# A transformer block on one core: gates of the second merge as filling work, and attention scores over the whole array

## The reference, cut to what matters

```python
for l in range(DEPTH):                       # 2 layers
    h = rmsnorm(x, norm_w[l])
    proj = h @ w_in[l]                       # q_b k_b v_b z_b gate_a gate_b ...
    y_a = gated_delta_branch(...)
    y_b = diff_attention_branch(q_b, k_b, v_b, z_b, ...)
    merged = sigmoid(gate_a) * (y_a @ w_pa[l]) + sigmoid(gate_b) * (y_b @ w_pb[l])
    x = x + merged @ w_out[l]

# diff_attention_branch, for each of 8 heads:
    q, k = partial_rope(q), partial_rope(k)  # two maps of 64 channels
    s = einsum('nbhqd,nbhkd->nbhqk', q, k)   # n = the map
    p = softmax(s)
    o = (p[0] - lam * p[1]) @ v
    y = rmsnorm(o, subln_w) * (1 - lambda_init) * silu(z)
```

## Time and profile before

| | |
|---|---|
| median of three runs | 3010.39 us |
| profiled execution | 3007.67 us |
| its span, first to last instruction | 3005.9 us |
| PE busy | 2952.6 us, 98% of the span |
| DVE, ACT, POOL busy | 57%, 47%, 15% |
| granted PE clock over the span | 0.999 |
| DMA, share of 16 engines | 22.7% in the queue of the loads |

### The profile page before, as it was taken

One profiled execution on the slowest core, in us unless ns is written; L12 is line 12 of the kernel. 1 busy time (PEld: TensorE's weight loads), 2 busy tenths in 40 slices (PEclk: granted clock), 3 DMA queues, 4 the chain that ended last, 5 costly groups with the idle time before them and its releaser, 6 DMA issues. The chain is left out here.

```text
span 3005.9 us, 51504 instructions
## 1 busy us (share of the span) xinstructions
PE 2952.6 (98%) x20584; PEld 2374.7 (79%) x20584; DVE 1716.1 (57%) x2610; ACT 1426.2 (47%) x2807; POOL 451.2 (15%) x288
## 2 busy tenths in 40 slices
PE   9999999999999999999999999999999999999999
PEld 6788788777787777877777877778888777788887
DVE  7766743776447777634676446554444555544443
ACT  4555543666334555534665345653223356632322
POOL 1555530000013445410000020000000100000000
PEclk9999999999999999999999999999999999999999
DMA  4121122212222112122221322212222222122222
GB/s 152 65 78 54 62 78 86 76 60 74 84 89 86 65 65 86 34 95 74 74 76 44 107 102 77 82 68 101 98 96 86 84 88 78 41 107 96 86 97 84
DMA packets 42692, 243.22 MB, mean 81 GB/s; under 512 B 6833, under 2 KB 7793, under 8 KB 17137
## 3 DMA queue, kind: packets, MB, share of 16 engines
q1 hardware_dynamic: 42480, 240.30, 22.7%
HBM read 233.36 MB, written 2.20 MB: 78 GB/s over the span
## 5 line engine op out<-in xcount | busy, mean ns | idle before, releaser
L320 PE MATMUL bank<-hT,ws 128*128 128x512 f32 x2112 | 875.6, 415 | 8.0 <-ACT rq L3182 2.5
L324 PE MATMUL bank<-hT,ws 128*128 128x512 f32 x2112 | 826.6, 391 | 0.0
L323 PE MATMUL bank<-hT,ws 128*128 128x512 f32 x2112 | 824.5, 390 | 0.0
L271 ACT ACTIVATE ws<-raw 128x2048 fp32r<-128x2048 f32 x172 | 328.8, 1912 | 296.1 <-PE bank L320 181.1
L320 PEld LDWEIGHTS bank<-hT,ws 128*128 128x128 f32 x2112 | 397.4, 188 | 91.0 <-issue 12.7
L324 PEld LDWEIGHTS bank<-hT,ws 128*128 128x128 f32 x2112 | 396.4, 188 | 87.1
L277 DVE TENSOR_TENSOR ws<-raw,ws 128x2048 fp32r<-128x2048 f32 x156 | 363.6, 2331 | 161.8 <-ACT ws L271 158.5
L323 PEld LDWEIGHTS bank<-hT,ws 128*128 128x128 f32 x2112 | 398.2, 189 | 66.8 <-issue 1.4
L1213 PE MATMUL bank<-uS,ws 128*128 128x512 f32 x512 | 199.2, 389 | 0.0
L1216 PE MATMUL bank<-uS,ws 128*128 128x512 f32 x512 | 199.2, 389 | 0.0
L1217 PE MATMUL bank<-uS,ws 128*128 128x512 f32 x512 | 199.2, 389 | 0.0
(11 more groups left out here) (388 smaller groups left out, 4887.2 us busy)
## 6 DMA issues: line engine op xcount, KB each, us to landing
raw<-in_w_ff SPq DMA_DIRECT2D x64, 1024.0 KB, 4.7
raw<-in_w_delta SPq DMA_DIRECT2D x32, 1024.0 KB, 4.7
raw<-in_w_diff SPq DMA_DIRECT2D x32, 1024.0 KB, 4.7
raw<-in_w_att SPq DMA_DIRECT2D x20, 1024.0 KB, 4.7
raw<-in_w_merge_a SPq DMA_DIRECT2D x16, 1024.0 KB, 4.8
raw<-in_w_merge_b SPq DMA_DIRECT2D x16, 1024.0 KB, 4.7
raw<-in_w_out SPq DMA_DIRECT2D x16, 1024.0 KB, 4.8
rows<-sum_rows SPq DMA_DIRECT2D x16, 512.0 KB, 5.7
```

What stands on the lines that cost most here:

```text
L271: act.activation(self.k.ws[:, c % 2, 0], self.k.raw[:, c % 2], ACT.Copy).then_inc(self.high_done, 1)
L320: first = pe.matmul(out, hi, x[:, 0, k], start=(begin and k == steps[0]), stop=False)
L323: pe.matmul(out, hi, x[:, 1, k], start=False, stop=False)
L324: last = pe.matmul(out, lo, x[:, 0, k], start=False, stop=(end and k == steps[-1]))
```

## The change

The scores become two matmuls per map over the full array: the stationary side holds a map's query high part in one half of the rows and its low part in the other (`QS`), the moving side the key's high part in both halves (`KH`), then the key's low part in both (`KL`). Two things follow. Splits of queries and keys are written in halves of 64 partitions, two instructions each where there was one. And six transfers of 64 x 512 fp32 per head put the parts into the other half of the partitions (`place_query`, `place_key`). The low parts now stand ahead of `weights` on DVE, the high parts ahead of the raw copies on ACT.

The filling work changes its counts: 28 steps, 9, then 7, so 44 steps are done when unit 0 begins. At its end it now holds four gate tiles at the full rate, copied to `gt`, and 7 steps of each of the first two `w_pb` tiles. The chunks of the merge are reordered (`MERGE_B_ORDER`), and chunk (1,0) and (1,1) are split inside the diff phase, the low part of (1,1) on POOL. `last_merge_phase` replaces `merge_phase`.

```diff
-GATES_AHEAD = 6
+MERGE_B_ORDER = ((0, 0), (0, 2), (1, 0), (1, 2), (0, 4), (1, 4), (0, 6), (1, 6))
+GATES_AHEAD, GATES_AHEAD_B = 6, 4
...
 @block.gpsimd
                 pool.memset(rot[:, :, :], 0.0).then_inc(cleared, 1)
+                following.low(pool, 1, 1)
...
 @block.sync
+                def place_query(h):
+                    sp.wait_ge(qk_ready, nth(h, 2, 0))
+                    for m in range(2):
+                        sp.dma_start(QS[MAPS[1 - m], h % 2, m].bitcast(F32), ql[MAPS[m]].bitcast(F32)).then_inc(placed[0], 16)
+                def place_key(h):
+                    sp.wait_ge(qk_high, nth(h, 2, 1))
+                    for m in range(2):
+                        sp.dma_start(KH[MAPS[1 - m], h % 2, m].bitcast(F32), KH[MAPS[m], h % 2, m].bitcast(F32)).then_inc(placed[1], 16)
+                    sp.wait_ge(qk_ready, nth(h, 2, 1))
+                    for m in range(2):
+                        sp.dma_start(KL[MAPS[1 - m], h % 2, m].bitcast(F32), KL[MAPS[m], h % 2, m].bitcast(F32)).then_inc(placed[1], 16)
...
                 for h in range(1, HEADS):
                     swap(h, 0)
                     refill(h, 1)
                     swap(h, 1)
+                    place_query(h)
+                    place_key(h)
                     if h + 1 < HEADS:
                         refill(h + 1, 0)
-                following.load_after(sp, 0, 0)
+                for n in range(4):
+                    following.load_after(sp, n // 2, n % 2)
...
 @block.tensor, stream()
-                    for _ in first_gates(k, pe, following, taken, 4 * HEADS):
+                    following.credit(pe)
+                    for n in range(GATES_AHEAD_B):
+                        x = n // 2
+                        if n % 2 == 0:
+                            following.ready(pe, 0, x)
+                        pe.wait_ge(taken, 4 * HEADS + n - 1)
+                        for last in following.product(pe, B[n % 2][:, :], x, n % 2, k.hT):
+                            if last is None:
+                                yield
+                        last.then_inc(tile, 1)
                         yield
-                        yield
-                    pe.wait_ge(p_ready, 2 * UNITS1)
-                    yield from first_merge(k, pe, following, MERGE_DIFF, yS, lambda t: pe.wait_ge(ylo, t + 1))
+                    following.ready(pe, 1, 0)
+                    for m in range(2):
+                        pe.wait_ge(taken, 4 * HEADS + GATES_AHEAD_B + m - 1)
+                        part = following.product(pe, B[m][:, :], 0, m, yS, steps=MERGE_FIRST, end=False)
+                        for t in MERGE_FIRST:
+                            pe.wait_ge(ylo, t + 1)
+                            next(part)
+                            yield
...
 @block.tensor, scores(u)
                     if n == 0:
                         pe.wait_ge(qk_ready, nth(h, 2, 1))
+                        pe.wait_ge(placed[0], 32 * (h + 1))
+                        pe.wait_ge(placed[1], 64 * (h + 1))
...
-                    for t, (a, b) in enumerate(((0, 0), (0, 1), (1, 0))):
-                        for m in range(2):
-                            hp = slice(64 * m, 64 * (m + 1))
-                            last = pe.matmul(B[SB + m][:, :], qk[hp, h % 2, 0, a, n * P:(n + 1) * P], qk[hp, h % 2, 1, b],
-                                             start=(t == 0), stop=(t == 2))
+                    for m in range(2):
+                        q = QS[:, h % 2, m, n * P:(n + 1) * P]
+                        pe.matmul(B[SB + m][:, :], q, KH[:, h % 2, m], start=True, stop=False)
+                        pe.matmul(B[SB + m][:, :], q, KL[:, h % 2, m], start=False, stop=True).then_inc(s_ready, 1)
...
                 fill = stream()
                 some(fill, 3 * KT + 4)
+                turn_v(0)
+                some(fill, KT + 1)
                 scores(0)
-                some(fill, KT - 4)
-                turn_v(0)
-                some(fill, KT)
+                some(fill, KT - 1)
...
 @block.scalar, in the loop over units
+                    if n in (1, 2) and more:
+                        qk_high_part(h + 1, n - 1)
                     if n < 3 and more:
                         raw_copy(h + 1, n)
-                    if n in (1, 2) and more:
-                        qk_high_part(h + 1, n - 1)
+                    elif not more:
+                        gate_copy(n)
...
+                    if n == 2 and not more:
+                        following.high(act, 1, 0)
...
                         if more:
+                            z_gate(h + 1)
                             v_turned(h + 1)
-                            z_gate(h + 1)
...
                 out_rms(HEADS - 1)
+                following.high(act, 1, 1)
                 high_part(HEADS - 1)
...
 @block.vector, in the loop over units
+                    if n in (1, 2) and more:
+                        qk_low_part(h + 1, n - 1)
                     if n == 1 and h > 0:
                         norm_out(h - 1)
                     if u + 1 < UNITS1:
                         weights(u + 1)
...
-                    if n in (1, 2) and more:
-                        qk_low_part(h + 1, n - 1)
...
+                    if n == 2 and not more:
+                        following.low(dve, 1, 0)
```

More of the change, by code:

```diff
@@ L391, in weight_chunks @@
             f.append(tile_pair(column_tile(w, (COL_VB + at, P)), column_tile(w, (COL_ZB + at, P))))
[L392 to L395, removed]
+        for chunks, order, sides in ((ma, MERGE_A_ORDER, ((w, COL_GA), (pa, 0))), (mb, MERGE_B_ORDER, ((w, COL_GB), (pb, 0)))):
+            for side, n in order:
+                m, at = sides[side]
+                chunks.append(tile_pair(column_tile(m, (at + n * P, P)), column_tile(m, (at + (n + 1) * P, P))))
         for n in range(0, KT, 2):
@@ L856, in gated_merge_phase, with last_merge_phase @@
     k.next_phase()
[L859 to L878, removed]
+def last_merge_phase(k, st, following, yS, macc, gt, mS, pairs=()):
     st.open()
@@ L881, in merge_phase @@
                                               "constants_loaded")
[L882 to L962, removed]
@@ L2426, in _ @@
                 swap(0, 1)
+                place_query(0)
+                place_key(0)
                 refill(1, 0)
@@ L2547, in raw_copy, with gate_copy @@
                     act.sem_inc(raw_ready, 1)
+                def gate_copy(n):
+                    act.wait_ge(tile, 4 * HEADS + n + 1)
+                    act.activation(gt[:, n], B[n % 2][:, :], ACT.Copy).then_inc(taken, 1)
                 def v_turned(h):
@@ L2556, in qk_high_part @@
                     act.wait_ge(qk_mixed, nth(h, 2, j))
-                    act.activation(qk[:, h % 2, j, 0], rq[:, j], ACT.Copy).then_inc(qk_high, 1)
+                    for m, hp in enumerate(MAPS):
+                        ins = act.activation((QS, KH)[j][hp, h % 2, m], rq[hp, j], ACT.Copy)
+                    ins.then_inc(qk_high, 1)
                 def z_gate(h):
@@ L2639, in qk_low_part @@
                     dve.wait_ge(qk_high, nth(h, 2, j))
-                    dve.tensor_tensor(qk[:, h % 2, j, 1], rq[:, j], qk[:, h % 2, j, 0].bitcast(F32), ALU.subtract).then_inc(qk_ready, 1)
+                    if j == 0 and h > 0:
+                        dve.wait_ge(placed[0], 32 * h)
+                    for m, hp in enumerate(MAPS):
+                        low = KL[hp, h % 2, m] if j else ql[hp]
+                        ins = dve.tensor_tensor(low, rq[hp, j], (QS, KH)[j][hp, h % 2, m].bitcast(F32), ALU.subtract)
+                    ins.then_inc(qk_ready, 1)
                 def maxes(u):
```

140 lines of the change are left out of this document (122 added, 18 removed).

## The result

The changed kernel takes 3107.5 us (median of 5 runs, 3103.6 to 3109.9), the kernel before 3011.3 beside it (3008.7 to 3013.1): a ratio of 1.032, 95% interval 1.0309 to 1.0332. That is 96 us slower; the forecast was 61 us slower, with a range up to 3100, so the time lies outside the range. The span of the profiled execution rose from 3005.9 to 3102.9 us, by 97.0.

What follows compares the result with a forecast made beforehand. PE, busy 98% of the span, was taken to bound the kernel. The terms -5 + 55 - 4.5 + 10 + 8 = +63.5 us on 3007.67 gave 3071, stated as 3072 us for the median; range 3042 to 3100.

Steps and rivals of the forecast that it cites:

- The wait in block 2: PE waits for the chunk's low part on DVE, 4.0 us in heads 1 to 6, 3.4 in head 0: +55 us.
- S: Start of the last filling matmul ahead of a unit's scores, from which the forecast counts times in that unit.
- Rival 2, the clock falls: PE returns at 1.2 GHz behind 16 waits, 2.8 us each: +45, about 3117; in a third, 3087; chance 0.12.
- Scores: Four full-array matmuls replace six paired half-row ones, saving 0.08 us per unit over 64 units: -5 us.
- the bound of -10: Far bound of the scores' saving, if the turning matmul also starts without its extra delay.
- Last head: PE's old waits at half-rate gates go, -4.5 us; new waits for merge chunks in blocks 0 and 2, +10 us.
- Phase boundary: At the barrier PE waits 5 us instead of 1, behind ACT's and POOL's late chunk (1,1): +8 us for both.
- At nothing: Priced at zero: key transfers covered by block 2's wait (+20 at most without it); block 3's silu gate in time.
- Rivals 1 and 3: Block 2: 1, only the softmax chain delays the chunk, about 3042, chance 0.2; 3, no wait, about 3000, 0.06.
- rival 1's 8.0: Block 2's chunk low part ends 8.0 us after S if DVE is free and only the softmax stands in the chain.

Runs made afterwards that it cites:

- forty: The changed kernel with 40 instead of 44 filling steps ahead of unit 0: 3007.7 us, ratio 0.9993.
- before_44: The kernel before the change with 44 instead of 40 filling steps ahead of unit 0, nothing else: 3112.1 us, ratio 1.0341.
- split_first: The changed kernel, 44 steps kept, with the chunk's low part in block 2 right behind the maxima on DVE: 3036.7 us, ratio 1.0087.
- best_old_scores: The changed kernel with 40 steps, ACT's chunk (1,1) split before the norm, raw copies first, but old half-array scores and no transfers: 3007.8 us.
- warm_half: The changed kernel with seven idle fp32 products on PE in the block 2 waits of heads 0 to 6: 3101.6 us, ratio 1.0306.

## Why the prediction was wrong

- **The wait in block 2, +55: right.** Measured 56.2. S + 4.7 for the reciprocal, 6.3 for the gating, 9.6 for the end of the low part were all met; head 0 waits 3.73, heads 1 to 6 3.74 to 4.42. forty and before_44 show the cause by taking the four steps out and putting them in, split_first by moving the low part.
- **The clock, left out of the sum: the step that failed.** "Rival 2, the clock falls" was given 0.12 and the sum nothing, on the ground that the longest wait of the trace, 2.48 us, kept the full clock. That row was one draw: the same wait lost the clock in four of twelve traces. It also says nothing of waits of 4 and 5 us, and falls followed the last heads' waits of 2.3 to 2.5 us too. The page of the Trainium skill weighed there ("TensorE: Matmul & The Clock Gate", part 1) said that idling halves the clock, and the trace now agrees: 0.53 and 0.64 in the windows behind the wait. The sum should have held a term for it. Its size in the rival (2.8 us for each of 16 waits, +45) was too high, because the lower clock held for part of the twelve matmuls only, 1.61 us in the wait shown; there were 20 such waits, and the estimate from the mean clock is 34 in all. The other terms came to 61.4 where 63.5 was summed, and 3072 + 34 = 3106 is 1.5 us under the measured 3107.5. A match that close is partly luck, since the 34 is good to some 3 us only.
- **Scores, -5: under-sized.** -8 by the distances: 0.07 us of it to the turning matmul, as forecast, and 0.05 behind it, which was named only as the bound of -10. best_old_scores bears it out, though its two differences (10.8 and 7.0) are too far apart to fix the size.
- **Last head, -4.5 and +10: right** (10.2).
- **Phase boundary, +8: right in size** (7.5), in part by luck. POOL's operation took 4.51 us and not the 4.95 reckoned with, and DVE's last one, 4.06 us long beside it, ended 0.56 us later still; the two nearly cancel. I had written "a collision could lengthen it" and priced nothing.
- **At nothing:** the transfers were indeed hidden behind the waits. Without that cover they cost 2.4 us (forty) to 8.3 (split_first), not up to 20, and nothing where the raw copies come first. The silu gate was hidden in the changed kernel; in before_44, with ACT's old order, it cost 5.7.
- **Rivals 1 and 3** are out: the rotation of the key ended at S + 1.2, not before S, and DVE reached the low part at S + 7.3, not before 3.3. What put its end 1.6 us above rival 1's 8.0 was mostly ACT, not DVE: from the maxima (731.65) to the exponentials (733.78) were 2.13 us instead of 0.73, since the key's high parts and raw copy stand between. The forecast had that order in its chain.
- **A slip of the sum.** 3071 and 2.7 for the median are 3074, not 3072. It changes nothing here.

What stays open: what decides whether the clock falls behind a wait of 2 to 3.6 us. It isn't the length alone, nor the work around the wait: the same code kept the clock in one execution and lost it in another, and no run here shows on what that hangs.

## What to carry to other kernels

When filling work is consumed in portions and the lead ahead of the loop isn't a whole number of units, count for every portion in which unit it begins and where its preparation stands on the other engines there; four steps more in that lead, one number, were worth 100 us here. With that number right the change was worth 3 us against the kernel before, within noise; with two operations of ACT moved as well, 13 to 14. Price a wait on TensorE with the slower matmuls behind it, and do so even if the trace shows no fall of the clock behind its own longest wait: one wait in one execution shows what can happen, not what will. A term that only a single row speaks against and that recurs 20 times belongs in the sum, not in a rival.

## What the runs showed of the hardware

- Behind most waits of 2.0 to 4.8 us PE's granted clock went to its lower level, sometimes only after PE had started again (two matmuls at full speed first, in warm_half), but not behind all: a wait of 3.56 us in the changed kernel kept the full clock, and one and the same wait of 2.48 us lost it in four of twelve traces. A fall cost up to 1.6 us behind the waits of block 2 in the changed kernel, 1.4 in the mean of the 14.
- A 128x512 DVE operation with two inputs in SBUF, 0.69 us by itself, took 4.06 and 4.12 us when it started about 1 us behind a 128x2048 one on POOL, and ended 0.5 to 0.6 us after it (837.79 against 837.23). The Trainium skill ("SBUF — State Buffer", section "SBUF: two separate sides") says that a DVE operation with two SBUF inputs and a GpSimd one that reads SBUF need the same port pair, which whoever starts first holds to the end of its instruction; the trace agrees with that here.
- Products on half the rows in pairs were no faster: three pairs took 1.22 us from the filling matmul ahead to the turning behind, four products over the whole array 1.15. Of the four distances one was 0.23 us, as between full products, and three were about 0.1 longer: into the first pair, from it to the second, and out of the last.
